# When the second half's weights are loaded, and in which order the sync queue ends the attention phase

## The reference

```python
for l in range(DEPTH):                                   # DEPTH = 2
    h = rms_norm(x, norm_g[l]); p = h @ w_in[l]          # (tokens, 1024) @ (1024, 3328)
    qa, ka, va, ga, qb, kb, vb, gb = split(p)
    attn = swa(qa, ka, va, sinks[l])                     # window 128, 8 heads of 64, 2 kv heads
    ret, S = retention(qb, kb, vb)                       # chunks of 128, 4 heads of 128 x 128
    x = x + concat(silu(ga) * attn, silu(gb) * rms_norm(ret)) @ w_out[l]
    # outputs: the last 128 k and v of the prompt, S, and for the samples
    # the k/v cache shifted by 4 tokens with the 4 new ones behind it, and S
```

## Time and profile before

| what | value |
|---|---|
| time, median of 3 executions | 1936.16 us (1933.39 to 1937.66) |
| the profiled execution: its time, its span | 1933.39 us, 1931.6 us |
| PE busy | 1796.7 us, 93% |
| DVE busy | 1385.2 us, 72% |
| ACT busy | 722.3 us, 37% |
| phase A of layer 0 ends, B0 begins | about 386 us |
| phase O of layer 0 | about 829 to 1022 us |
| phase A of layer 1 ends, B0 begins | about 1320 us |

### The profile page before, as it was taken

The page is one execution under the profiler, slowest core; times in us unless marked ns, Lnnn a source line. Parts: engine busy times, 40 slices in busy tenths (PEclk is TensorE's granted clock), DMA queues, the critical chain, the costliest instruction groups (busy, mean ns, idle before and its releaser), DMA issues.

```text
span 1931.6 us, 35859 instructions
## 1 busy us (share of the span) xinstructions
PE 1796.7 (93%) x11752; PEld 991.9 (51%) x11752; DVE 1385.2 (72%) x4744; ACT 722.3 (37%) x1841; POOL 68.7 (4%) x108
## 2 busy tenths in 40 slices
PE   0778899999999999987998999999999999999999
PEld 0345555655555555543444655555555555555444
DVE  4768999977665766676885899998766576667442
ACT  2556576632232222232442656665123222222010
POOL 3010000010000000011001000000100000000000
PEclk9999999999999999998999999999999999999999
DMA  5973545463002100079995233334400021004874
GB/s 150 204 188 72 98 93 109 82 152 120 11 11 101 64 11 8 25 197 235 235 243 155 52 72 77 75 76 98 155 12 11 27 93 54 11 11 127 201 217 142
DMA packets 353807, 196.66 MB, mean 102 GB/s; under 512 B 296625, under 2 KB 327537, under 8 KB 353553
## 3 DMA queue, kind: packets, MB, share of 16 engines
q1 hardware_dynamic: 343984, 159.89, 35.4%
q0 software_dynamic: 9728, 35.66, 5.7%
HBM read 88.75 MB, written 41.16 MB: 67 GB/s over the span
## 4 chain that ended last, share of the span: by engine, by line
PE 59%; DVE 22%; DMA 5%; ACT 4%; issue 4%; SPq 3%; DVEq 0%; ACTq 0%; POOL 0%; POOLq 0%
PE PB L514 24%; PE PA L514 23%; DMA r<-r 3%; DVE r L1060 2%; PE S L668 2%; PE OB L687 2%; DVE r L1017 2%; PE TK L657 2%; PE S L703 1%; PE OB L694 1%; DVE mix L1135 1%; DVE r L1022 1%; DVE w_mx L871 1%; DMA hT<-land 1%; SPq L2246 1%
## 5 line engine op out<-in xcount | busy, mean ns | idle before, releaser
L514 PE MATMUL PB<-w_a,hT 128*128 128x512 f16 (+1 forms) x1920 | 405.6, 362 | 0.0
L514 PE MATMUL PA<-w_a,hT 128*128 128x512 f16 (+1 forms) x1920 | 403.5, 361 | 1.0 <-DVE land L1003 1.0
L514 PEld LDWEIGHTS PB<-w_a,hT 128*128 (+1 forms) x1920 | 185.9, 99 | 179.2 <-issue 12.8
L514 PEld LDWEIGHTS PA<-w_a,hT 128*128 (+1 forms) x1920 | 186.5, 99 | 171.6 <-issue 4.1
L514 PE MATMUL PA<-w_b,r 128*128 128x512 f16 x768 | 178.5, 391 | 22.6 <-DMA r<-r 15.5
L1799 ACT ACTIVATE r<-OB 128x128 f32<-128x128 f32 (+1 forms) x136 | 36.4, 273 | 390.7 <-PE S L703 364.2
L514 PE MATMUL PA<-w_b,hT 128*128 128x512 f16 x768 | 177.9, 382 | 0.0
L514 PE MATMUL PB<-w_b,hT 128*128 128x512 f16 x768 | 176.3, 379 | 0.6 <-DVE r L1162 0.6
L514 PE MATMUL PB<-w_b,r 128*128 128x512 f16 x768 | 171.3, 379 | 0.0
L1182 DVE TENSOR_TENSOR r<-S,t_dec 128x256 f32<-128x256 f32 x64 | 27.2, 425 | 155.9 <-PE S L668 155.6
L514 PEld LDWEIGHTS PA<-w_b,r 128*128 128x128 f16 x768 | 75.9, 100 | 121.2 <-DMA r<-r 24.2
(11 more groups left out here) (258 smaller groups left out, 2896.5 us busy)
## 6 DMA issues: line engine op xcount, KB each, us to landing
out<-r SPq DMA_DIRECT2D x40, 512.0 KB, 4.7
r<-mixed SPq DMA_DIRECT2D x32, 512.0 KB, 4.0
w_b<-in_w_in POOLq DMA_DIRECT2D x16, 512.0 KB, 8.5
mixed<-mix SPq DMA_DIRECT2D x32, 256.0 KB, 2.0
mixed<-mix SPq DMA_DIRECT2D x64, 128.0 KB, 1.8
w_a<-in_w_in POOLq DMA_DIRECT2D x16, 512.0 KB, 8.1
w_b<-in_w_out POOLq DMA_DIRECT2D x16, 512.0 KB, 7.1
r<-in_x_prompt SPq DMA_DIRECT2D x16, 512.0 KB, 4.7
```

Of the source, the lines that this page charges most:

```text
L514: last = nc.tensor.matmul(out[0:s.rows, 0:n], lhs, w16(ph, k, p, wpart), start=(k == 0 and part == 0 and wpart == 0), stop=(k == KT - 1 an ...
```

## The change

Four things are edited. POOL no longer waits for the prob transposes and the B0 states before it loads B1's weights (both layers). POOL's loads of layer 1's A weights wait for lower counts of O pieces. DVE takes four of the maxima of those weights, and `w_top`, at step 6 of phase O, and none at step 7. At the end of phase A, SPq stores the keys and values after the two mixed stores and the state loads, and in layer 0 the cache copy now stands ahead of the state loads too.

```diff
@@ DVE, phase O @@
-                    if not last and 4 <= c < 8:
-                        for q in (2 * c - 8, 2 * c - 7):
+                    if not last and 4 <= c < 7:
+                        for q in ((0, 1), (2, 3), (4, 5, 6, 7))[c - 4]:
                             w_absmax(L + 1, "A", q)
-                    if not last and c == 7:
+                    if not last and c == 6:
                         w_top(L + 1, "A")
                     if not last and c == 7:
                         w_scale(L + 1, "A")
@@ POOL, weight loads @@
                         for q in range(KT):
-                            pool.wait_ge(dve_piece, free + (2, 3, 5, 6, 7, 8, 10, 11)[q])
+                            pool.wait_ge(dve_piece, free + 1 + q)
                             load_weights(G, kind, nl, (q,))
                     else:
                         pool.wait_ge(dve_piece, free)
-                        if kind == "B1":
-                            for g in range(2):
-                                pool.wait_ge(a_tp[g], 16 * (L + 1) * TILES)
-                            pool.wait_ge(sts_ld, (L * 2 + 1) * 32)
                         load_weights(G, kind, nl)
@@ SPq, end of phase A @@
                 prob_T(L, E - 1, 1)
                 prob_T(L, E, 0)
+                store_mix("A", L, E - 1)
+                prob_T(L, E, 1)
+                store_mix("A", L, E)
+                if L == 0:
+                    for o, i in ((nk_s, cache_k), (nv_s, cache_v)):
+                        for l in range(DEPTH):
+                            sp.dma_start(o[l, :, 0:WINDOW - DEC_SEQ].rearrange("b w g d -> b (w g d)"),
+                                         i[l, :, DEC_SEQ:WINDOW].rearrange("b w g d -> b (w g d)")).then_inc(kc_out, 16)
+                for g in range(2):
+                    sp.wait_ge(a_tp[g], 16 * (L + 1) * TILES)
+                load_states("B0", L)
                 for o, c0 in ((nk_p, A_W), (nv_p, A_W + KV_W)):
                     sp.dma_start(at(o).rearrange("o n w g d -> (o n w) (g d)"),
                                  land[:, E.par, c0:c0 + KV_W]).then_inc(kv_out, 16)
-                store_mix("A", L, E - 1)
-                prob_T(L, E, 1)
-                store_mix("A", L, E)
-                for g in range(2):
-                    sp.wait_ge(a_tp[g], 16 * (L + 1) * TILES)
-                load_states("B0", L)
                 if not last:
                     load_gains(L + 1)
@@ SPq, phase B0 @@
-                    if ph == "B0" and L == 0:
-                        for o, i in ((nk_s, cache_k), (nv_s, cache_v)):
...
```

## The result

The changed kernel takes 1990.32 us (median of 4, 1988.82 to 1991.69) against 1936.05 for the kernel before: 54.3 us more, a ratio of 1.0282 with the 95% interval 1.0264 to 1.03. It is slower. The forecast was 41.5 us more and 1975, range 1950 to 1992, so the time lies 2 us inside the upper end; the prediction's own list of chances had given times over 1986 a chance of 0.13. The profiled execution took 1986.21 us with a span of 1984.4, so the two spans differ by 52.8 us.

The account below looks back on a forecast made before the run. PE, busy 1796.7 of 1931.6 us, was taken as the bound. 14 + 7.5 + 18 + 6 - 4 = 41.5 us on the profiled 1933.39 made 1974.9; it said 1975 us, range 1950 to 1992.

Parts of the forecast that it names:

- times over 1986: Whole kernel: the case with each term at its upper end, 67 us more, 2000 us; chance 0.13.
- The stores, layer 0: Seam from A to B0: key and value stores behind mix store, cache copies and state loads delay ACT and PE 14 us.
- the upper bound of 16.7: Layer 0 seam: stores queue behind the data of copies (9.7 us) and states (3.3), then land in 3.3: 16.7 us late.
- a sign of being wrong: Layer 0 seam: the stores land soon after issue in spite of the copies; no size given.
- the lower bound: Layer 0 seam: stores delayed only by issues ahead on SPq, no transfer hindering another; second lands 9.6 us late.
- The stores, layer 1: Layer 1 seam, no cache copies: stores behind the state loads come 7.5 us late, up to 11.
- The loads beside the transposes: Both seams: B1's early weight loads delay tile E - 1's prob transposes 9 us a layer, 18 us in all.
- one transpose's extra 9.4 us: An h transpose issued into eight B0 loads landed after 13.9 us against 4.5; taken as the nearest case.
- my upper bound: Seam transposes: 2.8 us of their own; standing behind all eight B1 loads makes one 13 us later.
- The clock: Three new PE waits at the seams, each followed by slow matmuls costing 2 us: 6 us (0 to 9).
- Phase O: Layer 0: earlier A loads use idle engine time, 4 us of gain; bounds 14.6 of gain and 4 of loss.
- Cover that I counted on: After the seam's delay PE runs phase B0 without a gap, so nothing gives the time back.

Follow-up runs that it names:

- Both single parts: Each against the kernel before: SPq's new order alone, 25.3 us more; POOL's early B1 loads alone, 33.5 more; the phase O edits alone, 5.3 less.

## Why the prediction was right, and where its sizes were off

Its direction held, and the places at which PE came to wait were those forecast. The total came 12 us over the forecast because one term was mis-sized, and in one step the way to the right size was another than written. By its own steps:

**The stores, layer 0: 14 us.** The lateness was 16.8, at the upper bound of 16.7, but not in the way that the bound was built. It had the stores queued behind the data of the copies and the states after their issue. The prediction named as a sign of being wrong that the stores land soon after issue in spite of the copies, and that is what they did (4.7 and 3.6 us). The time went into SPq's issues, which ended 13.6 us after the store of the mix had begun, where the lower bound had 7.5. That the two ways give the same number is in part luck: the states' second issue ended when the copies' data did, and the 9.7 us for these were right. The number of engines that the copies use fits the Trainium skill ("DMA: Bandwidth & Descriptors", section "Why a DMA increments its semaphore by 16 and not by 1", which is where the rule that the prediction cites stands): 8 rows, 8 engines, and 49.7% busy. The copies alone were worth 8.5 to 11. Of the 16.8, PE felt 15.1: the 1.7 us of slow matmuls that the old wait caused were paid already, and the new ones ran while the chain over ACT and DVE was late anyway.

**The stores, layer 1: 7.5 us.** 7.4: DVE's mix of E ends at 1395.73, so that ACT could begin at 1395.8, and it begins at 1403.20.

**The loads beside the transposes: 18 us.** This is the term that was mis-sized. The two seams lost 15.2 and 18.7 us up to b_T of T0 (L657), 33.9 in all, and the experiment with POOL's edit alone measured 33.5, against 22 in the forecast with the slow clock. I took one transpose's extra 9.4 us as the price. There the loads had begun 6 us before it; here they begin 1 us before, and it had almost all of them to share turns with. It landed 19.5 and 22.7 us after its issue. That is even more than my upper bound (2.8 + 13 + what a landing takes), since that bound took the engines to keep their pace, and the stretches above show them down to 145 GB/s while the two meet; why they fell isn't shown. The Trainium skill ("DMA: Bandwidth & Descriptors", section "Queues, rings and completion order") describes turns of one packet each, and from 401 to 406 us the trace agrees, 430 against 432. That rule pointed at the right end of the range, and I stayed 4 us below it.

**The clock: 6 us.** Next to nothing. DVE's softmax of E, which waits for the same transpose, began 15.2 and 18.4 us later than before, and that is the loss of the two seams within 0.4 us: the slow matmuls behind PE's waits ran while PE would have waited for DVE's chain anyway. At the stores none came on top either. Matmuls at the lower clock did stand behind each of the four waits; what was wrong is to count them on the path.

**Phase O: 4 us of gain.** 4.4 between the traces, 5.3 by the medians. The split was the other way round: PE's waits fell only from 19.6 us to 18.7, and the matmuls at the lower clock from 7.4 to 4.1 us above 5.35 (two such places in place of the three in the earlier trace rows). As I had said, the wait ahead of T2 grew (6.23 to 10.73) and the later ones shrank, from 13.4 to 7.9 together. The moved maxima cost nothing that the trace shows. One reading was wrong, and the sum doesn't hang on it: the last two loads move by three pieces, which is one and a half steps and not two and a half.

**Cover that I counted on.** Nothing behind the seams gave time back; the sum of the places is the difference of the spans within 0.8 us. Both single parts together, 25.3 + 33.5 - 5.3 = 53.5, give the 54.3 of the whole, so within the intervals they don't overlap.

## What to carry to other kernels

Before a bulk load is started earlier because its buffer is free, look for a small-packet transfer that somebody waits for in the same microseconds: the two take turns by packets, not by time, and here a transpose of 4 us then landed after 20. A wait that looks superfluous for correctness may be there for that. A store that frees a buffer belongs ahead of everything on its queue that nobody awaits, copies of few and long rows above all. Look at how long the issues ahead of a store take as well as at its landing: here the copies made the stores late before they were issued. Where the transfer engines are full, moving loads about in the stretch moves the waits: here it gained 5.3 us, with 3.1 us of idle engine time within reach.

## What the runs showed of the hardware

- Two queues with work moved the same number of packets: 430 of 1.57 MB against 432 of 0.11 MB in 5 us. In the first 2 us of the meeting they didn't (64 against 1049).
- With four copies on half of the engines ahead of them, the second of two state loads (512 KB each) took 5.6 and 6.0 us to issue (two kernels) and the store behind it 3.0, against 2.5 and 0.6 without the copies. The stores landed 3.5 to 4.8 us after their issue in all three.
- As a transpose joined running loads, the total fell from 314 to 145 GB/s with full engines, and it was 155 GB/s with only four loads queued. I had not expected that, and why it is so stays open.
- The price of meeting is far from linear in the loads: 1.5, 22.5 and 33.5 us over both layers for one, four and eight early loads in each.
- Two executions of one pattern differ: the first transpose of E - 1 beside the same eight loads landed after 19.5, 20.4, 21.0, 22.7, 23.0 and 23.0 us, in two layers of three kernels.
